# A block model in float32 on one core: the sums of the modulation vector's last four sixths, made in the wait before the token mixer instead of inside it

## Chip, cores and metric

One core of one Trainium2 chip runs one launch. The metric is device time in microseconds (us), lower is better; a run counts with the time of its only core.

## What is computed

Two blocks one after the other on 256 tokens of width 1024. The first has two layers, each attention and a squared-ReLU MLP with layer norms. The second is what the change touches: a vector c gives a modulation vector of 6 x 1024 numbers, whose sixths shift, scale and gate a token mixer and a mixture of experts.

```python
def second_block(...):
    c_act = jax.nn.silu(c)
    mod = (c_act @ w_ada[l] + b_ada[l])[:, None, :]
    sh1, sc1, g1, sh2, sc2, g2 = jnp.split(mod, 6, axis=-1)
    u = modulate(rmsnorm(h, norm1[l]), sh1, sc1)
    h = h + g1 * token_mixer(u, ...)
    u = modulate(rmsnorm(h, norm2[l]), sh2, sc2)
    h = h + g2 * hier_moe(u, ...)
    return rmsnorm(h, final_norm)
```

The mixer projects u to retention queries, keys, values and gates and to latents of a second attention, and merges both branches under two sigmoid gates; the experts are routed per token.

## The kernel before

The kernel is one program with one hand-written instruction list for each engine: `block.sync` (all weight loads), `block.gpsimd` (small and modulation loads), `block.tensor`, `block.scalar` and `block.vector`. Semaphores, named in the table `S`, tie the lists together; on each engine the instructions run in the written order. Here PE is TensorE, ACT is ScalarE, DVE is VectorE, and the order around the change is the order of the calls in those three functions.

**Weights.** Each weight block of 1 MB lands in one of four ring slots. ACT rounds it to `w_hi` (`high`, L1197), DVE writes the rest `w_lo` (`low`, L1570), and PE makes every product with three matmuls (`product`, L555 to L557) for float32-like precision. The activations come the same way: PE transposes a 128-token tile (`transposes`, L523), ACT copies it, DVE splits it to `x_hi` and `x_lo`. `tokens_out` is one projection of all 256 tokens to 1024 columns (four blocks, 96 matmuls) into the four PSUM banks of `acc`; ACT then empties the banks (`banks_out`, L1341), and the next projection waits with `freed=` for that.

**Modulation.** During both MLPs DVE accumulates c_act times the rows of w_ada in `mod` (128 partitions x 6144). The sum over the partitions is a matmul with ones. The first two sixths (shift and scale of the mixer) are needed by feature: 32 one-column matmul passes (L829) leave them in `pp` bank 0, and DVE makes `modc` from them (L1859, L1861). The last four sixths are needed by token in every partition: `mod_rows(part)` on PE multiplies a 128x512 piece of `mod` by ones into a bank of `pp` (L839, two passes for each piece, 8 pieces), and `mod_rows(part)` on ACT copies the bank back over the same piece (L1348), counting `mod_done`. Both banks of `pp` are shared. Before the change `mod_rows(0)` to `mod_rows(3)`, two pieces each, stand inside the mixer: after the projections RG (retention gate), GR and GM (the two merge gates), and RO (retention output).

**Between the second MLP and the mixer.** DVE takes the last layer norm and the RMS norm of both tiles (`last_sum`, `row_stats`, `last_norm`, `mixer_rows`), ACT takes the square roots (`norm_root`, L1308; `mixer_root`, L1362), PE transposes each tile when its `mixer_rows` is out (`r_out`), ACT applies `modc` on the way out of PSUM (`mixer_input`, L1142), DVE splits (L1557, L1558). Then the first projection of the mixer, B_C, begins. The experts come after the mixer, in a hardware loop whose weights (L397) stream while PE multiplies (L1065, L1049, L1105).

Of the kernel before, what the change touches and what calls it, by code (L numbers as in the profile page):

```python
# [27 lines left out]
LN_EPS = 1e-5  # L28
# [30 lines left out]
B_C = 96  # L59
# [44 lines left out]
def program(nc, A):  # L104
    f32, i32, f32r = mybir.dt.float32, mybir.dt.int32, mybir.dt.float32r
    ALU, ACT, AX = mybir.AluOpType, mybir.ActivationFunctionType, mybir.AxisListType
    ctx = ExitStack()
    with ctx:
# [46 lines left out]
        def con(name, rows=128):  # L155
            if name in LATE_AT:
                a, b = LATE_AT[name]
                if name == "mask":
                    return late_mask
                return stage[:, :, :].rearrange("p a b -> p (a b)")[:, a:b]  # L160
            a, b = CONST_AT[name]
            return consts[0:rows, a:b]
# [350 lines left out]
        def _(pe):  # L513
# [26 lines left out]
            def input_split():  # L540

                if groups[0] - 1 in PLAIN:
                    transposed()
                else:
                    inputs[0] += 4
                    pe.wait_ge(S["x_split"], inputs[0])
# [25 lines left out]
            def tokens_out(b, freed=None, by_tile=False, before=lambda i, j: None, cuts=(0, 512, 1024)):  # L572

                def part(i, j, q):
                    k, half = divmod(j, 2)
                    kt = 2 * i + k
                    n = cuts[half + 1] - cuts[half]
                    return product(acc[:, 2 * q + half, 0:n], x_parts(kt, slice(q * 128, (q + 1) * 128)),
                                   w_parts(b + i, k, slice(cuts[half], cuts[half + 1])),
                                   start=(kt == 0), stop=(kt == 7))  # L580

                for i in range(3 if by_tile else 4):
                    for j in range(4):
                        before(i, j)
                        if j % 2 == 0:
                            half_ready(b + i, j // 2)
                        if freed and i == 0 and j < 2:
                            pe.wait_ge(S[freed], 2 * (j + 1))
                        for q in range(QT):
                            last = part(i, j, q)  # L590
                        if j % 2 == 1:
                            last.then_inc(S["half_used"], 1)
                if by_tile:
                    before(3, 0)
                    for j in range(4):
                        if j % 2 == 0:
                            half_ready(b + 3, j // 2)
                        last = part(3, j, 0)
                    last.then_inc(S["tile_ready"], 1)
                    for j in range(4):  # L600
                        last = part(3, j, 1)
                        if j % 2 == 1:
                            last.then_inc(S["half_used"], 1)
# [226 lines left out]
                                     con("ones")[:, 0:1], start=True, stop=True)  # L830
            last.then_inc(S["mod_mm"], 1)

            def mod_rows(part):

                if part:
                    pe.wait_ge(S["mod_done"], 2 * part)
                for half in range(2):
                    at = 2048 + 1024 * part + 512 * half
                    pe.matmul(pp[:, half, :], con("ones"), mod[:, at:at + 512], start=True, stop=True)\  # L839
                        .then_inc(S["mod_mm"], 1)  # L840


            for q in range(QT):
                pe.wait_ge(S["r_out"], q + 1)
                for half in range(2):
                    transposes([(128 * j, o_tm[:, q, (4 * half + j) * 128:(4 * half + j + 1) * 128])
                                for j in range(4)])
            input_split()

            tokens_out(B_C, cuts=(0, 384, 704))  # L850

            def rqk(i):

# [17 lines left out]
            n = 0  # L871
# [108 lines left out]
            pe.wait_ge(S["rq_done"], 4)  # L980
            pe.wait_ge(S["rk_done"], 4)
            tokens_out(B_RG)
            mod_rows(0)
            tokens_out(B_GR, freed="rg_done")
            mod_rows(1)
            tokens_out(B_GM, freed="gr_done")
            mod_rows(2)
            for q in range(QT):
                pe.wait_ge(S["yret_ready"], q + 1)
                tile_to_feature_major(o_tm, q)  # L990
            input_split()
            tokens_out(B_RO, freed="gm_done")
            mod_rows(3)
            to_feature_major(o_mla)
            input_split()
            tokens_out(B_MO, freed="ret_merged")
# [126 lines left out]
        def _(act):  # L1123
# [182 lines left out]
            def norm_root(i, q):  # L1306
                act.wait_ge(S["ln_stat"], QT * i + q + 1)
                act.activation(rstd[:, q:q + 1], sr[:, q:q + 1], ACT.Sqrt).then_inc(S["ln_rstd"], 1)  # L1308
# [32 lines left out]
                        act.activation(dst[:, q, 512 * half:512 * half + 512], acc[:, 2 * q + half, :], function)\  # L1341
                            .then_inc(done, 1)

            def mod_rows(part):
                for half in range(2):
                    at = 2048 + 1024 * part + 512 * half
                    act.wait_ge(S["mod_mm"], 2 * part + half + 2)
                    act.activation(mod[:, at:at + 512], pp[:, half, :], ACT.Copy).then_inc(S["mod_done"], 1)  # L1348

            for layer in range(2):  # L1350
                attention(layer)
# [8 lines left out]
            def mixer_root(q):  # L1360
                act.wait_ge(S["r_stat"], q + 1)
                act.activation(rstd[:, q:q + 1], sr[:, q:q + 1], ACT.Sqrt).then_inc(S["r_rstd"], 1)  # L1362

            def mixer_input(*halves):
                to_input(lambda f: modc[:, 1, f:f + 1], lambda f: modc[:, 0, f:f + 1], halves)

            mixer_root(0)
            norm_root(3, 1)
            act.wait_ge(S["modc_done"], 1)
            mixer_input(0, 1)  # L1370
            mixer_root(1)
            mixer_input(0, 1)

            high(B_C + 1, n=5)
            used(B_C + 3)
            for q in range(QT):
                act.activation(lat[:, q, 0:384], acc[:, 2 * q, 0:384], ACT.Copy)
# [57 lines left out]
            used(B_RG + 3)  # L1435
            banks_out(rg, ACT.Silu, S["rg_done"])
            high(B_GR + 1)
            mod_rows(0)
            high(B_GR + 2, n=3)
            used(B_GR + 3)  # L1440
            banks_out(gate_r, ACT.Sigmoid, S["gr_done"])
            high(B_GM + 1)
            mod_rows(1)
            high(B_GM + 2, n=3)
            used(B_GM + 3)
            banks_out(gate_m, ACT.Sigmoid, S["gm_done"])
            mod_rows(2)
            to_input_plain()
            high(B_RO + 1, n=4)
            mod_rows(3)  # L1450
            to_input_plain()
            high(B_MO + 1, n=4)
            to_input_plain()
# [58 lines left out]
        def _(dve):  # L1512
# [12 lines left out]
            def used(b):  # L1525

                dve.wait_ge(S["half_used"], half_index(b, 1) + 1)
# [300 lines left out]
            def last_sum(q):  # L1828
                bank = acc[:, 2 * q:2 * q + 2, :].rearrange("p a b -> p (a b)")
                link(dve.scalar_tensor_tensor(o_tm[:, q, :], h_tm[:, q, :], ALPHA, bank, ALU.mult, ALU.add))  # L1830
# [9 lines left out]
            def mixer_rows(q):  # L1840
# [9 lines left out]
            row_stats(0, o_tm[:, 0, :], LN_EPS, S["ln_stat"])  # L1850
            last_norm(0)
            row_stats(0, h_tm[:, 0, :], EPS, S["r_stat"], rms=True)
            used(b)
            last_sum(1)
            row_stats(1, o_tm[:, 1, :], LN_EPS, S["ln_stat"])
            mixer_rows(0)

            dve.wait_ge(S["mod_mm"], 1)
            link(dve.tensor_copy(modc[:, :, :].rearrange("p a b -> p (a b)"), pp[:, 0, 0:16]))  # L1859
            at = VEC["norm1_2"][0]  # L1860
            dve.scalar_tensor_tensor(modc[:, 1, :], modc[:, 1, :], 1.0, vec[:, at:at + 8], ALU.add, ALU.mult)\  # L1861
                .then_inc(S["modc_done"], 1)
            last_norm(1)
            row_stats(1, h_tm[:, 1, :], EPS, S["r_stat"], rms=True)
            mixer_rows(1)
# [413 lines left out]
```

## Time and profile before

| what | value |
|---|---|
| median of 3 runs | 1378.13 us (1377.3 to 1379.1) |
| time of the profiled execution | 1377.12 us |
| its span in the trace | 1375.3 us |
| mean granted TensorE clock | 0.932 of full speed |
| TensorE matmul busy | 1229.9 us, 89% of the span |
| VectorE busy | 747.7 us, 54% |
| ScalarE busy | 519.3 us, 38% |
| GpSimd busy | 55.4 us, 4% |
| mean DMA rate | 208 GB/s |

Times in the trace count from the start of the span. An engine's busy time says how long it worked, not that it was waited for: that is read from the idle time before an instruction and from what ended it. A granted clock of 1.00 is TensorE at 2.4 GHz, 0.50 is 1.2 GHz.

### The profile page before, as it was taken

To read this page: it belongs to the slowest core of one execution; us is meant where nothing else is said; L and a number is where in the kernel's file an instruction comes from. 1 tells how busy PE (TensorE), PEld (TensorE's weight loads), DVE (VectorE), ACT (ScalarE), POOL (GpSimd) and SP (SyncE) were. 2 spreads that over 40 slices of the span, in tenths; PEclk is the share of its full clock that TensorE was granted. 3 is DMA by queue.
4 is the path that set the end of the run, shared out by engine and by line. 5 is a ranking of instruction groups with operands and counts; after the bars stand their busy time and mean duration, and the time that the engine had idled before them with its cause. 6 is when DMAs were issued, how large, how long until landed. Compare 5 with 4: busy or idle time off the path is not lost. (4 is left out here: it accounts for less than half of the span.)

```text
span 1375.3 us, 18670 instructions
## 1 busy us (share of the span) xinstructions
PE 1229.9 (89%) x7419; PEld 1013.4 (74%) x7419; DVE 747.7 (54%) x1256; ACT 519.3 (38%) x854; POOL 55.4 (4%) x98
## 2 busy tenths in 40 slices
PE   7788599999799869999969999999988699999994
PEld 5786489999698759999958778878766566666653
DVE  3366567777656566777775334554455722222223
ACT  3356444444445443444434322344432222222221
POOL 6000000010000000000000000000000000000000
PEclk9899789999899979999979968999998599999998
DMA  9933248788563216978724412635457199999992
GB/s 272 284 104 94 90 137 291 277 279 283 172 214 119 96 61 213 322 280 286 248 88 100 153 41 83 203 107 185 151 192 236 61 311 367 366 367 367 366 367 83
DMA packets 176069, 286.08 MB, mean 208 GB/s; under 512 B 11613, under 2 KB 137818, under 8 KB 175616
## 3 DMA queue, kind: packets, MB, share of 16 engines
q1 hardware_dynamic: 165616, 248.76, 54.1%
q0 software_dynamic: 10384, 36.37, 8.3%
q8 instruction: 46, 0.75, 0.2%
q14 instruction: 23, 0.19, 0.0%
HBM read 282.92 MB, written 2.20 MB: 207 GB/s over the span
## 5 line engine op out<-in xcount | busy, mean ns | idle before, releaser
L1570 DVE TENSOR_TENSOR w_lo<-ring,w_hi 128x1024 fp32r<-128x1024 f32 (+1 forms) x272 | 320.0, 1210 | 163.8 <-ACT w_hi L1197 156.5
L1197 ACT ACTIVATE w_hi<-ring 128x1024 fp32r<-128x1024 f32 (+1 forms) x272 | 277.9, 1050 | 180.6 <-PE acc L557 159.3
L555 PE MATMUL pp<-x_hi,w_hi 128*128 128x256 f32 x896 | 264.3, 295 | 14.3 <-DVE w_lo L1570 7.5
L556 PE MATMUL pp<-x_lo,w_hi 128*128 128x256 f32 x896 | 259.9, 290 | 0.0
L557 PE MATMUL pp<-x_hi,w_lo 128*128 128x256 f32 x896 | 259.7, 290 | 0.0
L555 PEld LDWEIGHTS pp<-x_hi,w_hi 128*128 128x128 f32 x896 | 178.5, 199 | 22.7 <-issue 14.0
L556 PEld LDWEIGHTS pp<-x_lo,w_hi 128*128 128x128 f32 x896 | 178.7, 199 | 1.4 <-issue 0.2
L557 PEld LDWEIGHTS pp<-x_hi,w_lo 128*128 128x128 f32 x896 | 178.3, 199 | 0.0
L555 PE MATMUL acc<-w_hi,x_hi 128*128 128x512 f32 (+2 forms) x384 | 156.8, 408 | 23.6 <-DVE x_lo L1544 7.1
L556 PE MATMUL acc<-w_lo,x_hi 128*128 128x512 f32 (+2 forms) x384 | 153.4, 399 | 0.0
L557 PE MATMUL acc<-w_hi,x_lo 128*128 128x512 f32 (+2 forms) x384 | 153.0, 398 | 0.0
L555 PEld LDWEIGHTS acc<-w_hi,x_hi 128*128 128x128 f32 x384 | 76.2, 198 | 45.3 <-DVE x_lo L1544 9.6
L555 PE MATMUL acc<-w_hi,hid_hi 128*128 128x512 f32 x256 | 100.0, 391 | 0.0
L556 PE MATMUL acc<-w_lo,hid_hi 128*128 128x512 f32 x256 | 100.0, 390 | 0.0
L557 PE MATMUL acc<-w_hi,hid_lo 128*128 128x512 f32 x256 | 99.6, 389 | 0.0
L557 PEld LDWEIGHTS acc<-w_hi,x_lo 128*128 128x128 f32 x384 | 75.8, 197 | 15.3
L556 PEld LDWEIGHTS acc<-w_lo,x_hi 128*128 128x128 f32 x384 | 75.9, 198 | 14.3
L1331 ACT ACTIVATE scr<-pp 128x512 f32<-128x512 f32 x32 | 19.1, 598 | 152.5 <-PE pp L557 152.5
L1793 DVE TENSOR_TENSOR scr<-scr 128x512 f32<-128x512 f32 x32 | 22.1, 692 | 81.7 <-ACT scr L1331 81.6
L1584 DVE SCALAR_TENSOR_TENSOR mod<-stage,act_c,mod 128x1024 f32<-128x1024 f32 x48 | 61.4, 1278 | 0.0
L523 PE MATMUL tp<-consts,o_tm 128*128 128x128 f32 x142 | 26.5, 341 | 38.1 <-DVE o_tm L1769 14.2
L1065 PE MATMUL pp<-ring,k_t 128*64 128x256 f32 x512 | 57.1, 379 | 3.5 <-DMA ring<-in_w_dram 3.5
(344 smaller groups left out, 1731.9 us busy)
## 6 DMA issues: line engine op xcount, KB each, us to landing
ring<-in_w_up_dram SPq DMA_DIRECT2D x32, 1024.0 KB, 5.3
ring<-in_w_down_dram SPq DMA_DIRECT2D x32, 1024.0 KB, 6.9
ring<-in_w_dram SPq DMA_DIRECT2D x32, 1024.0 KB, 12.7
stage<-in_w_ada_dram POOLq DMA_DIRECT2D x48, 512.0 KB, 6.5
ring<-in_w_in_dram SPq DMA_DIRECT2D x24, 1024.0 KB, 5.1
big<-in_w_dram SPq DMA_DIRECT2D x24, 1024.0 KB, 11.2
ring<-in_w_in_a_dram SPq DMA_DIRECT2D x12, 1024.0 KB, 14.0
ring<-in_w_kv_shared_dram SPq DMA_DIRECT2D x8, 1024.0 KB, 5.8
```

What stands on the lines that cost most here:

```text
L523: last = pe.transpose(tp[:, g % 2, off:off + 128], src, ident)
L555: pe.matmul(out, lhs[0], rhs[0], start=start, stop=False)
L556: pe.matmul(out, lhs[0], rhs[1], start=False, stop=False)
L557: return pe.matmul(out, lhs[1], rhs[0], start=False, stop=stop)
L1065: last = pe.matmul(up_bank[64 * e:64 * e + 64, 256 * w:256 * w + 256], xe[:, kt, x], e_ring[6 * pair + 2 * w + e][:, 256 * kt:256 * kt + 256],
L1197: act.activation(shaped(high_half(bb, k), raw), raw, ACT.Copy).then_inc(S["hi_ready"], 1)
L1331: act.activation(relu[:, v % 2, :], pp[:, v % 2, :], ACT.Relu).then_inc(S["relu_done"], 1)
L1570: dve.tensor_tensor(shaped(low_half(bb, k), raw), raw, shaped(high_half(bb, k), raw), ALU.subtract).then_inc(S["lo_ready"], 1)
L1584: dve.scalar_tensor_tensor(part, stage[:, i % 2, :], act_c[:, k:k + 1], part, ALU.mult, ALU.add)\
L1793: dve.tensor_tensor(h, h, h, ALU.mult).then_inc(S["sq_done"], 1)
```

## The change

PE's and ACT's `mod_rows` take a range of pieces instead of a sixth's number, and alternate the banks of `pp` starting with bank 1. On PE the pieces 0 and 1 come right after the one-column matmuls, 2 to 6 between the transposes of tile 0 and tile 1, 7 after those of tile 1; piece 1 waits for `modc_done`, since bank 0 holds the sums for `modc` until then. On ACT the copies 0 and 1 stand ahead of the last `norm_root`, 2 to 6 between the modulated copies of tile 0 and the square root of tile 1, 7 between the first and the second block of B_C. On DVE `modc` and `mixer_rows(0)` move ahead of `last_sum(1)`. The four calls inside the mixer go, and PE waits for all eight copies before it next writes `pp`.

```diff
--- before.py
+++ after.py
@@ -830,24 +830,28 @@
                                      con("ones")[:, 0:1], start=True, stop=True)
             last.then_inc(S["mod_mm"], 1)
 
-            def mod_rows(part):
-
-                if part:
-                    pe.wait_ge(S["mod_done"], 2 * part)
-                for half in range(2):
-                    at = 2048 + 1024 * part + 512 * half
-                    pe.matmul(pp[:, half, :], con("ones"), mod[:, at:at + 512], start=True, stop=True)\
+            def mod_rows(start, end):
+
+                for i in range(start, end):
+                    if i == 1:
+                        pe.wait_ge(S["modc_done"], 1)
+                    elif i >= 2:
+                        pe.wait_ge(S["mod_done"], i - 1)
+                    at = 2048 + 512 * i
+                    pe.matmul(pp[:, (i + 1) % 2, :], con("ones"), mod[:, at:at + 512], start=True, stop=True)\
                         .then_inc(S["mod_mm"], 1)
 
-
+            mod_rows(0, 2)
             for q in range(QT):
                 pe.wait_ge(S["r_out"], q + 1)
                 for half in range(2):
                     transposes([(128 * j, o_tm[:, q, (4 * half + j) * 128:(4 * half + j + 1) * 128])
                                 for j in range(4)])
+                mod_rows(2 + 5 * q, 7 + q)
             input_split()
 
             tokens_out(B_C, cuts=(0, 384, 704))
+            pe.wait_ge(S["mod_done"], 8)
 
             def rqk(i):
 
@@ -980,17 +984,13 @@
             pe.wait_ge(S["rq_done"], 4)
             pe.wait_ge(S["rk_done"], 4)
             tokens_out(B_RG)
-            mod_rows(0)
             tokens_out(B_GR, freed="rg_done")
-            mod_rows(1)
             tokens_out(B_GM, freed="gr_done")
-            mod_rows(2)
             for q in range(QT):
                 pe.wait_ge(S["yret_ready"], q + 1)
                 tile_to_feature_major(o_tm, q)
             input_split()
             tokens_out(B_RO, freed="gm_done")
-            mod_rows(3)
             to_feature_major(o_mla)
             input_split()
             tokens_out(B_MO, freed="ret_merged")
@@ -1341,11 +1341,12 @@
                         act.activation(dst[:, q, 512 * half:512 * half + 512], acc[:, 2 * q + half, :], function)\
                             .then_inc(done, 1)
 
-            def mod_rows(part):
-                for half in range(2):
-                    at = 2048 + 1024 * part + 512 * half
-                    act.wait_ge(S["mod_mm"], 2 * part + half + 2)
-                    act.activation(mod[:, at:at + 512], pp[:, half, :], ACT.Copy).then_inc(S["mod_done"], 1)
+            def mod_rows(start, end):
+
+                for i in range(start, end):
+                    at = 2048 + 512 * i
+                    act.wait_ge(S["mod_mm"], i + 2)
+                    act.activation(mod[:, at:at + 512], pp[:, (i + 1) % 2, :], ACT.Copy).then_inc(S["mod_done"], 1)
 
             for layer in range(2):
                 attention(layer)
@@ -1365,13 +1366,16 @@
                 to_input(lambda f: modc[:, 1, f:f + 1], lambda f: modc[:, 0, f:f + 1], halves)
 
             mixer_root(0)
+            mod_rows(0, 2)
             norm_root(3, 1)
             act.wait_ge(S["modc_done"], 1)
             mixer_input(0, 1)
+            mod_rows(2, 7)
             mixer_root(1)
             mixer_input(0, 1)
-
-            high(B_C + 1, n=5)
+            high(B_C + 1)
+            mod_rows(7, 8)
+            high(B_C + 2, n=4)
             used(B_C + 3)
             for q in range(QT):
                 act.activation(lat[:, q, 0:384], acc[:, 2 * q, 0:384], ACT.Copy)
@@ -1435,19 +1439,15 @@
             used(B_RG + 3)
             banks_out(rg, ACT.Silu, S["rg_done"])
             high(B_GR + 1)
-            mod_rows(0)
             high(B_GR + 2, n=3)
             used(B_GR + 3)
             banks_out(gate_r, ACT.Sigmoid, S["gr_done"])
             high(B_GM + 1)
-            mod_rows(1)
             high(B_GM + 2, n=3)
             used(B_GM + 3)
             banks_out(gate_m, ACT.Sigmoid, S["gm_done"])
-            mod_rows(2)
             to_input_plain()
             high(B_RO + 1, n=4)
-            mod_rows(3)
             to_input_plain()
             high(B_MO + 1, n=4)
             to_input_plain()
@@ -1850,16 +1850,15 @@
             row_stats(0, o_tm[:, 0, :], LN_EPS, S["ln_stat"])
             last_norm(0)
             row_stats(0, h_tm[:, 0, :], EPS, S["r_stat"], rms=True)
-            used(b)
-            last_sum(1)
-            row_stats(1, o_tm[:, 1, :], LN_EPS, S["ln_stat"])
-            mixer_rows(0)
-
             dve.wait_ge(S["mod_mm"], 1)
             link(dve.tensor_copy(modc[:, :, :].rearrange("p a b -> p (a b)"), pp[:, 0, 0:16]))
             at = VEC["norm1_2"][0]
             dve.scalar_tensor_tensor(modc[:, 1, :], modc[:, 1, :], 1.0, vec[:, at:at + 8], ALU.add, ALU.mult)\
                 .then_inc(S["modc_done"], 1)
+            mixer_rows(0)
+            used(b)
+            last_sum(1)
+            row_stats(1, o_tm[:, 1, :], LN_EPS, S["ln_stat"])
             last_norm(1)
             row_stats(1, h_tm[:, 1, :], EPS, S["r_stat"], rms=True)
             mixer_rows(1)
```

The list of PE's instructions between the second MLP and the first projection of the mixer (L841 is L839 before, the pieces' matmuls; L523 the transposes of `o_tm`):

```order
 L829 MATMUL pp<-consts,mod 128x1 x16
-L523 MATMUL tp<-consts,o_tm 128x128 x16
+L841 MATMUL pp<-mod,consts 128x512 x2
+L523 MATMUL tp<-consts,o_tm 128x128 x8
+L841 MATMUL pp<-mod,consts 128x512 x5
+L523 MATMUL tp<-consts,o_tm 128x128 x8
+L841 MATMUL pp<-mod,consts 128x512
 L555 MATMUL acc<-w_hi,x_hi 128x384
```

All eight pieces now stand ahead of B_C: two before the first tile's transposes, five between the tiles, one after.

The same place on ACT (L1349 is L1348 before, a piece's copy; L1363 is L1362 before, the root of the mixer's norm; L1308 the root of the layer norm; L1142 the modulated copies of a tile):

```order
 L1308 ACTIVATE rstd<-sr 128x1
-L1362 ACTIVATE rstd<-sr 128x1
+L1363 ACTIVATE rstd<-sr 128x1
+L1349 ACTIVATE mod<-pp 128x512 x2
 L1308 ACTIVATE rstd<-sr 128x1
 L1142 ACTIVATE scr<-tp,modc 128x128 x8
-L1362 ACTIVATE rstd<-sr 128x1
+L1349 ACTIVATE mod<-pp 128x512 x5
+L1363 ACTIVATE rstd<-sr 128x1
 L1142 ACTIVATE scr<-tp,modc 128x128 x8
```

The root of tile 1 followed the modulated copies of tile 0 directly; now five copies, each of which needs its matmul, stand between them.

ACT inside the mixer, from the emptying of GR's banks (first row) over GM's to the copies that start RO's input (last row):

```order
 L1341 ACTIVATE big<-acc 128x512 x4
-L1197 ACTIVATE w_hi<-ring 128x1024 x2
-L1348 ACTIVATE mod<-pp 128x512 x2
-L1197 ACTIVATE w_hi<-ring 128x1024 x6
+L1197 ACTIVATE w_hi<-ring 128x1024 x8
 L1341 ACTIVATE big<-acc 128x512 x4
-L1348 ACTIVATE mod<-pp 128x512 x2
 L1172 ACTIVATE x_hi<-tp 128x4x128 x4
```

The copies of pieces no longer stand between the emptying of GM's banks and the first copy of RO's input.

## Rows read from the trace of the kernel before

**Rows 1.** Chain of waits, mixer and experts: start us, us, what:

```profile
922.70 1.72 PE pp L839 x4
...
1099.39 7.13 PE pp L1065 x64
...
1296.25 11.86 DMA ring<-in_w_dram
```

**Rows 2.** Timeline of PE, MLP to mixer: start, us, operation, [idle before <-releaser]:

```profile
694.08 4.03 PE L829 MATMUL pp<-consts,mod 128*128 128x1 f32 x32
703.31 1.97 PE L523 MATMUL tp<-consts,o_tm 128*128 128x128 f32 x8 [5.20 <-DVE o_tm L1842]
709.34 1.97 PE L523 MATMUL tp<-consts,o_tm 128*128 128x128 f32 x8 [4.06 <-DVE o_tm L1842]
714.69 0.69 PE L555 MATMUL acc<-w_hi,x_hi 128*128 128x384 f32 x1 [3.38 <-DVE x_lo L1558]
```

**Rows 3.** Timeline of DVE, the same stretch:

```profile
699.46 1.20 DVE L1830 SCALAR_TENSOR_TENSOR o_tm<-h_tm,acc 128x1024 f32<-128x1024 f32 x1
...
702.52 0.73 DVE L1842 TENSOR_SCALAR o_tm<-h_tm,rstd 128x1024 f32<-128x1024 f32 x1
703.17 0.17 DVE L1859 COPY modc<-pp 128x16 f32<-128x16 f32 x1
...
708.53 0.75 DVE L1842 TENSOR_SCALAR o_tm<-h_tm,rstd 128x1024 f32<-128x1024 f32 x1 [0.27 <-ACT rstd L1362]
```

**Rows 4.** Timeline of ACT, the same stretch:

```profile
699.57 0.20 ACT L1362 ACTIVATE rstd<-sr 128x1 f32<-128x1 f32 x1 [4.50 <-DVE sr L1756]
702.64 0.20 ACT L1308 ACTIVATE rstd<-sr 128x1 f32<-128x1 f32 x1 [2.86 <-DVE sr L1756]
704.55 2.90 ACT L1142 ACTIVATE scr<-tp,modc 128x128 f32<-128x128 f32 x8 [1.71 <-PE tp L523]
708.29 0.20 ACT L1362 ACTIVATE rstd<-sr 128x1 f32<-128x1 f32 x1 [0.85 <-DVE sr L1756]
...
718.29 0.80 ACT L1197 ACTIVATE w_hi<-ring 128x704 fp32r<-128x704 f32 x1 [3.48 <-PE acc L557]
```

**Rows 5.** Windows: us, busy (x) of PE, PEld, DVE, ACT, POOL, then PEclk, DMA:

```profile
698.00:703.00 5.00, 0.12 (x1) 0.03 (x1) 4.72 (x13) 0.41 (x2) 0.00 (x0) 0.50 0.00 0
...
714.69:717.60 2.91, 2.91 (x10) 2.91 (x11) 1.55 (x2) 0.12 (x1) 0.00 (x0) 0.50 0.10 12
```

**Rows 6.** Timeline of PE, end of RG to GR:

```profile
922.53 1.88 PE L839 MATMUL pp<-mod,consts 128*128 128x512 f32 x4
...
924.48 0.40 PE L556 MATMUL acc<-w_lo,x_hi 128*128 128x512 f32 x1
924.72 0.40 PE L557 MATMUL acc<-w_hi,x_lo 128*128 128x512 f32 x1
```

**Rows 7.** Timeline of ACT, end of RG to GR:

```profile
922.73 2.07 ACT L1341 ACTIVATE big<-acc 128x512 f32<-128x512 f32 x4 [3.08 <-PE acc L557]
```

**Rows 8.** Timeline of ACT, end of GM to RO:

```profile
971.72 1.12 ACT L1348 ACTIVATE mod<-pp 128x512 f32<-128x512 f32 x2
972.68 1.15 ACT L1172 ACTIVATE x_hi<-tp 128x512 fp32r<-128x512 f32 x2
```

**Rows 9.** Timeline of PE, first matmuls of RO, and where they speed up:

```profile
976.84 0.66 PE L555 MATMUL acc<-w_hi,x_hi 128*128 128x512 f32 x1 [1.48 <-DVE x_lo L1544]
980.28 0.47 PE L557 MATMUL acc<-w_hi,x_lo 128*128 128x512 f32 x1
```

**Rows 10.** Timeline of DVE, end of RO to MO:

```profile
1000.53 2.48 DVE L2002 TENSOR_TENSOR q_t<-acc,big 128x512 f32<-128x512 f32 x4 [3.13 <-PE acc L557]
1003.36 1.29 DVE L1544 TENSOR_TENSOR x_lo<-tp,x_hi 128x512 fp32r<-128x512 f32 x2 [0.35 <-ACT x_hi L1172]
```

**Rows 11.** Timeline of PE, end of RO to MO:

```profile
1000.33 1.88 PE L839 MATMUL pp<-mod,consts 128*128 128x512 f32 x4
...
1006.77 0.50 PE L555 MATMUL acc<-w_hi,x_hi 128*128 128x512 f32 x1 [1.41 <-DVE x_lo L1544]
```

## Prediction

> **What bounds the kernel now.** I read the chain of waits first: it tells which engine's work sets the end. In the mixer it runs through PE, with the piece matmuls on it: four passes after RG are 1.72 us of it [rows 1]. So each of the eight pieces, two passes each, looks like 0.86 us of path. In the experts the chain is PE's passes over the streamed weights and late in the loop a wait of 11.86 us for a load [rows 1]. Both begin with the loop at 1099.39, so what the mixer gains or loses arrives at the end unchanged.
>
> Then the stretch between second MLP and mixer, on three engines. PE ends its one-column sums at 694.08 + 4.03 = 698.11 and starts B_C at 714.69; between them are two groups of transposes, each released by DVE's `mixer_rows` [rows 2]. DVE is the bound: only 0.27 us idle stands before its last `mixer_rows`, released by ACT's root [rows 3]. ACT idles 4.50, 2.86, 1.71 and 0.85 us before its steps there [rows 4]. PE's clock is at half speed, 0.50, from 698, and B_C's first 2.91 us run at it too [rows 5]. This is the space into which the pieces go.
>
> **What leaves the mixer.** Each removal is costed by what PE would wait for without it.
>
> After RG: PE cannot write the first banks of GR before ACT has emptied two. ACT starts at 922.73; four copies in 2.07 us at 0.60 us each [rows 7] (the last begins 1.47 us after the first, 0.49 us apart) put the second's end at 922.73 + 0.49 + 0.60 = 923.8, and GR could start at about 923.9. Now the pieces stream from 922.53, and GR's second pass starts at 924.48, 0.24 us before its third [rows 6], so the first effectively at 924.25. Gain 0.35 us, not 1.72: the pieces stood in a wait for PSUM that would be there without them. After GR the pattern is the same: 0.35 us.
>
> After GM, PE's next need is RO's input, which ACT copies. ACT's two piece copies start at 971.72, the first copy of RO's input at 972.68 [rows 8]. Without them the latter moves up 0.96 us, and DVE's split and RO with it: 0.96 us.
>
> After RO, DVE has four merges from 1000.53, 2.48 us, ending at 1003.0, and the first split starts at 1003.36 after a wait of 0.35 us for ACT's copy, itself behind the two piece copies [rows 10]. Without them DVE goes on at 1003.0: 0.35 us.
>
> Sum: 0.35 + 0.35 + 0.96 + 0.35 = **2.0 us off**. Bounds: 1.2 us (the first two give nothing, if emptying costs some tenths more) and 2.6 us.
>
> **What comes into the wait.** DVE's work is the same in another order. `modc` and `mixer_rows(0)` stand before `last_sum(1)`, which starts at 699.46 now, so `mixer_rows(0)` starts near 699.9 instead of 702.52 [rows 3]. Its transposes could follow at 700.7, were PE not busy with piece 1. Step by step:
> - PE: piece 0 from 698.1; piece 1 only after `modc`, 699.9. A piece is 0.86 us at full clock, so an estimated 1.72 at half. At half: both done at 701.6, transposes of tile 0 (1.97 us, rows 2) to 703.6.
> - ACT: root at 699.57, two copies (0.60 us each) by 702.4. The next root waits for tile 1's statistics. They come now at 702.64 - 0.04 = 702.60 [rows 4] and later by `mixer_rows(0)` and `modc`, some 1.0 us: root done 703.85. Then the eight modulated copies, 2.90 us [rows 4]: 706.8.
> - Pieces 2 and 3 are in their banks by 707.1 at the latest; ACT's copies free the first bank at 707.4. Piece 4 therefore starts at 707.45, whatever the clock, and 4, 5, 6 follow each other.
> - At full clock: 707.45 + 3 x 0.86 = 710.0, then the last copy and the root, 0.2 + 0.6 + 0.2: 711.0. At half: 707.45 + 3 x 1.72 = 712.6, root done 713.6. Today the root is done at 708.29 + 0.20 = 708.49 [rows 4].
>
> Behind that root everything of tile 1 queues: DVE's `mixer_rows(1)`, and on DVE behind it the splits of both tiles, then PE and B_C, 6.2 us from root to B_C today (708.49 to 714.69, rows 4 and 2) and then. So B_C starts **2.5 us later at full clock, 5.1 at half**. The trace has the clock low in all of this stretch, but pieces 2 and 3 give PE 3.4 us of dense work, and B_C's start shows the clock rising after 2.91 us of such [rows 5]. I take one of the three waiting pieces at half and two at full: 3.4 us. PE and ACT, idle there today, become the bound.
>
> Piece 7 costs nothing: PE has it while DVE splits tile 1, ACT in the 3.48 us idle before B_C's second block [rows 4]. PE's wait for eight copies comes after B_C's 96 matmuls and is met. Loads are issued in the same order and follow the weights' use; none is moved.
>
> **The clock.** Pieces were PE's dense work in its pauses. RO's first nine passes start from 976.84 to 980.28 at half clock, 0.43 us apart instead of 0.23 [rows 9]: 1.6 us lost. MO, after a like pause, starts at nearly full clock: its first pass takes 0.50 [rows 11]. Its last piece ends at 1000.33 + 1.72 = 1002.05 today, 4.7 us ahead of MO [rows 11]. Without pieces the last dense pass ends at 1000.5 and MO starts at about 1006.4: 5.9 us of transposes and idleness. RO's pause today is at least 4.6 us, from the start of the second piece's copy at 972.2 [rows 8] to 976.84. Ends: nothing, or RO's loss, 1.6 us. The nearest row is RO's, but MO's own says it may hold: I take 0.9 us. At B_C's start, low for 2.91 us today, the ends are no change and a gain of 1.45 us. The Trainium skill says ("TensorE: Matmul & The Clock Gate", section "Why this matters for your kernels") that long idle gaps between bursts of matmuls drop the clock and that keeping PE busy holds it up. By that rule B_C would start at full clock, and the sum would be 1.45 us lower. Row against it: transposes and a tail of DVE work of 6.2 us still lie between piece 6 and B_C, as long as the pause after which RO is slow, so I take no change.
>
> **Sum**: 3.4 - 2.0 + 0.9 + 0 = +2.3 us. The profiled execution took 1377.12 us and would take 1379.4; the median of the runs shown, 1378.13, is 1.0 above it, so against the median the forecast is **1380.4 us**. A measurement of this kernel can tell about 0.2%, 2.8 us, from no change.
>
> **Rivals.**
> 1. Slow clock throughout. The three waiting pieces run at half speed (+5.1) and MO starts slow (+1.6), with 2.0 off: +4.7 us, **1382.8**. For it: 0.50 in the whole stretch now. It decides if ACT's last root before B_C ends later than 712 and MO's first passes are 0.43 apart.
> 2. The pieces keep the clock up. Waiting pieces at full clock (+2.5), B_C at full clock from its start (-1.45), MO unharmed, 2.0 off: -0.95 us, **1377.2**, no change to a measurement. It decides if the granted clock is 1.00 when B_C starts. Against it: the 6.2 us tail. It is what the rule of the Trainium skill named above would make of this stretch.
> 3. The pieces were real path and the wait hides the new ones better than my steps say. PE's eight pieces come off in full, 8 x 0.86 = 6.9 us, with +3.4 in the wait: -3.5 us, **1374.6**, faster. The chain of waits speaks for it [rows 1]; ACT's emptying that ends at 923.8 speaks against it [rows 7]. It decides if GR starts as soon as RG ends.
> 4. The change doesn't do what it says (`modc` or a bank not free, so pieces queue in B_C): PE would idle after B_C for the eighth copy. Nothing in the rows makes that copy late; priced at up to +2 us more, it is inside rival 1's range.
>
> **Chances.** Forecast 0.50, of which 0.30 lies within 0.2% and 0.20 above; rival 1 (with 4) 0.22; rival 2 0.14; rival 3 0.14. Faster by over 0.2%: 0.14. Within: 0.30 + 0.14 = 0.44. Slower: 0.20 + 0.22 = 0.42. The range for 8 in 10 runs from just below rival 2 to above rival 1 with its bounds (5.1 - 1.2 + 1.6 = +5.5): **1376.0 to 1383.8**; it leaves out most of rival 3.
>
> **What would show it.** Right: in the stretch before B_C, idle of DVE before its last `mixer_rows` grows from 0.27 to 2.5 to 5 us, ended by ACT's root; that root stands behind five piece copies; GR and GM start about 1.4 us after the projection before them instead of 1.7, PE idle between; RO's first input copy follows the emptying directly; MO's first passes are slower. Wrong: the gap from the end of the MLP to B_C no longer than today, or PE running through from RG to GR without a pause, or the clock at 1.00 at B_C's start.

## The result, and the profile after

The changed kernel takes **1383.83 us** (median of 7 runs, 1382.52 to 1385.56), the kernel before in the same session 1377.30 us (7 runs). The ratio is 1.0049, 95% interval 1.0037 to 1.0061: 6.5 us slower. The profiled execution took 1383.83 us with a span of 1382.0 us, 6.7 us over the span before; mean granted clock 0.930.

Section 1 of the page of the changed kernel, busy us and share of the span:

```profile
PE 1237.2 (90%) x7419; PEld 1016.6 (74%) x7419; DVE 748.5 (54%) x1256; ACT 519.9 (38%) x854; POOL 55.4 (4%) x98
```

Every engine ran as many instructions as before, but PE's are 7.3 us longer in sum, more than the whole difference. That already points at PE's clock, not only at waits.

Timeline of PE, end of the second MLP to B_C, in the changed kernel (to be held against [rows 2]; L841 are the pieces):

```profile
694.68 3.63 PE L829 MATMUL pp<-consts,mod 128*128 128x1 f32 x32
698.17 1.10 PE L841 MATMUL pp<-mod,consts 128*128 128x512 f32 x2
700.48 2.08 PE L841 MATMUL pp<-mod,consts 128*128 128x512 f32 x2 [1.20 <-DVE modc L1856]
702.34 1.92 PE L523 MATMUL tp<-consts,o_tm 128*128 128x128 f32 x8
704.05 2.89 PE L841 MATMUL pp<-mod,consts 128*128 128x512 f32 x4
707.81 2.94 PE L841 MATMUL pp<-mod,consts 128*128 128x512 f32 x6 [0.87 <-ACT mod L1349]
712.32 1.10 PE L523 MATMUL tp<-consts,o_tm 128*128 128x128 f32 x8 [1.57 <-DVE o_tm L1842]
...
717.50 0.69 PE L555 MATMUL acc<-w_hi,x_hi 128*128 128x384 f32 x1 [3.22 <-DVE x_lo L1558]
```

The first row starts 0.60 us later than before, ahead of anything the change touches. From there to B_C it is 22.82 us, before 20.61: **2.2 us** more. Pieces 4 to 6 (x6) wait for ACT's copies.

Timeline of ACT between the tiles, and DVE's last `mixer_rows` (against [rows 4] and [rows 3]):

```profile
707.13 1.12 ACT L1349 ACTIVATE mod<-pp 128x512 f32<-128x512 f32 x2
708.98 0.60 ACT L1349 ACTIVATE mod<-pp 128x512 f32<-128x512 f32 x1 [0.73 <-PE pp L841]
709.84 0.60 ACT L1349 ACTIVATE mod<-pp 128x512 f32<-128x512 f32 x1 [0.26 <-PE pp L841]
710.79 0.60 ACT L1349 ACTIVATE mod<-pp 128x512 f32<-128x512 f32 x1 [0.36 <-PE pp L841]
711.28 0.19 ACT L1363 ACTIVATE rstd<-sr 128x1 f32<-128x1 f32 x1
...
711.51 0.76 DVE L1842 TENSOR_SCALAR o_tm<-h_tm,rstd 128x1024 f32<-128x1024 f32 x1 [2.55 <-ACT rstd L1363]
```

The chain of the prediction is there link by link: the root of tile 1 stands behind five copies, and DVE's idle time before its last `mixer_rows` grew from 0.27 to 2.55 us.

Windows of the changed kernel: from the copies of pieces 2 and 3 on (first row), the pieces between the tiles, the last 1.2 us before B_C, then B_C's, RO's and MO's first passes, and the last weight load's matmuls (columns as in [rows 5]; the figure after POOL's is the clock):

```profile
706.10:716.30 10.20, 5.74 (x18) 2.11 (x16) 6.62 (x15) 6.97 (x19) 0.54 (x1) 1.00 0.07 19
709.00:712.00 3.00, 1.75 (x4) 0.30 (x2) 0.49 (x1) 1.86 (x4) 0.00 (x0) 1.00 0.00 0
716.30:717.50 1.20, 0.00 (x0) 0.00 (x1) 1.17 (x3) 1.20 (x3) 0.00 (x0) 0.51 0.00 0
...
717.50:723.10 5.60, 5.60 (x18) 5.60 (x19) 2.34 (x3) 1.39 (x3) 0.00 (x0) 0.50 0.53 158
978.20:982.60 4.40, 4.36 (x10) 3.47 (x11) 2.36 (x2) 1.15 (x2) 0.00 (x0) 0.50 0.20 19
1008.20:1013.30 5.10, 5.04 (x12) 3.98 (x13) 2.37 (x3) 1.17 (x2) 0.00 (x0) 0.50 0.19 48
1347.60:1351.20 3.60, 3.60 (x18) 2.55 (x20) 0.00 (x0) 0.00 (x0) 0.00 (x0) 0.53 0.77 306
```

The clock is at 1.00 while the waiting pieces run and down again before B_C begins. B_C's passes are slow for 5.6 us (before 2.91, [rows 5]), RO's for 4.4 (before 3.4), MO's for 5.1 where before they began almost at speed [rows 11].

Timeline of PE in the mixer: the last pass of RG and the first two of GR, then around the inputs of RO and MO:

```profile
924.73 0.39 PE L557 MATMUL acc<-w_hi,x_lo 128*128 128x512 f32 x1
926.39 0.47 PE L555 MATMUL acc<-w_hi,x_hi 128*128 128x512 f32 x1 [1.27 <-ACT big L1341]
926.70 0.40 PE L556 MATMUL acc<-w_lo,x_hi 128*128 128x512 f32 x1
...
971.58 1.03 PE L523 MATMUL tp<-consts,o_tm 128*128 128x128 f32 x8
975.21 1.62 PE L523 MATMUL tp<-consts,o_tm 128*128 128x128 f32 x8 [2.59 <-DVE x_lo L1544]
978.24 0.80 PE L555 MATMUL acc<-w_hi,x_hi 128*128 128x512 f32 x1 [1.41 <-DVE x_lo L1544]
...
1002.13 1.03 PE L523 MATMUL tp<-consts,mod 128*128 128x128 f32 x8
1005.46 1.38 PE L523 MATMUL tp<-consts,mod 128*128 128x128 f32 x8 [2.30 <-DVE x_lo L1544]
1008.26 0.80 PE L555 MATMUL acc<-w_hi,x_hi 128*128 128x512 f32 x1 [1.41 <-DVE x_lo L1544]
```

Where pieces stood after RG, PE now idles 1.27 us until ACT has emptied the banks. RO begins 6.66 us after GM's passes (978.24 - 971.58), before 7.24 (976.84 less 969.60, where the pieces began); MO 6.13 after RO's, before 6.44 [rows 11]. The last RG pass and the first GR pass of the kernel before, for the comparison:

```profile
922.30 0.40 PE L557 MATMUL acc<-w_hi,x_lo 128*128 128x512 f32 x1
...
923.96 0.68 PE L555 MATMUL acc<-w_hi,x_hi 128*128 128x512 f32 x1
```

The 6.7 us add up along PE's list. Each row is the time from the start of one marked pass to the start of the next, read from the timelines of both traces (differences from the unrounded times):

| stretch | before | changed | difference |
|---|---|---|---|
| start of the span to the one-column sums | 694.1 | 694.7 | +0.6 |
| to B_C's first pass | 20.6 | 22.8 | +2.2 |
| to the first matmul of UQ (B_C, RQK) | 32.5 | 33.7 | +1.2 |
| to the last matmul of retention | 152.4 | 150.8 | -1.6 |
| to RO's first pass (RG, GR, GM) | 77.3 | 76.2 | -1.0 |
| to MO's first pass (RO) | 29.9 | 30.0 | +0.1 |
| to WO's first pass (MO) | 31.1 | 33.5 | +2.3 |
| to the router's first matmul (WO) | 31.6 | 32.4 | +0.8 |
| to the experts' first matmul | 29.8 | 30.3 | +0.4 |
| to the experts' last weight matmul | 246.5 | 248.1 | +1.7 |
| to the end of the span | 29.4 | 29.5 | 0.0 |

From retention to the router the pieces were taken off, and the stretch became 2.1 us longer (170.0 to 172.1).

### The profile page after: what moved, and what is told of

It is laid out like the page before. It is cut to its first block and busy times, and to the rows that moved or that the text cites. A ratio compares the mean times of both kernels' runs of the same rounds, so it can differ in the third digit from the quotient of the medians.

```text
span 1382.0 us, 18671 instructions
## 1 busy us (share of the span) xinstructions
PE 1237.2 (90%) x7419; PEld 1016.6 (74%) x7419; DVE 748.5 (54%) x1256; ACT 519.9 (38%) x854; POOL 55.4 (4%) x98
## 5 line engine op out<-in xcount | busy, mean ns | idle before, releaser
L2180 DVE SCALAR_TENSOR_TENSOR w_lo<-tp,slot_gate,w_hi 128x512 fp32r<-128x512 f32 x32 | 24.0, 751 | 66.3 <-ACT w_hi L1496 42.6
```

The lines of the kernel that those rows point to most:

```text
L2180: dve.scalar_tensor_tensor(y_lo[:, half, :], y_bank[half], slot_gate[:, 0:1], y_hi[:, half, :], ALU.mult, ALU.subtract).then_inc(S[f"y{hal ...
```

## The experiments

The questions: is it the wait or the clock, and what did the pieces in the mixer really cost? All ratios are against runs of the kernel before on the same chip.

**No pieces at all.** The calls of `mod_rows` go from PE and ACT, and DVE's wait for them. This kernel leaves the last four sixths of the vector unsummed, so its output is not the model's; it serves for timing alone:

```diff
             tokens_out(B_RG)
-            mod_rows(0)
             tokens_out(B_GR, freed="rg_done")
-            mod_rows(1)
             tokens_out(B_GM, freed="gr_done")
-            mod_rows(2)
...
-            dve.wait_ge(S["mod_done"], 8)
```

> The kernel before with the eight pieces left out on PE and ACT altogether (the last four sixths of the modulation vector are not summed over the partitions; nothing takes their place in the wait). Theory A, clock: the pieces in the mixer cost only 2.0 us of path, and they kept the clock up in the pauses before RO and MO, so that without them both start at half clock more often: 0 to +3 us against before, with a granted clock of 0.5 at MO's first passes. Theory B, the wait alone: taking them out of the mixer gains its 2 us and the clock's differences there are chance: -2 us. Theory C, the pieces were real path: -6.9 us.

1381.16 us against 1377.76, ratio 1.0018 (1.0006 to 1.0031). Eight matmuls and eight copies less, and the kernel is not faster but slower, by 2.5 us. In its trace RO and MO both start at half clock, and the way from retention to the router is 172.2 us, as in the changed kernel (172.1) and not as before (170.0). This is theory A's outcome; B and C are out. One part of its time has nothing to do with PE: behind the last instruction of DVE the span goes on for 3.1 us, in the kernel before for 4.0. The other kernel without pieces shows the same, all ten kernels with pieces are like before. Why the store of the output ends sooner there is not shown. Without this 1.0 us the loss would be about 3.5 us.

**The changed kernel with its pauses filled.** Six matmuls into an unused bank:

```diff
+            def fill(count):
+                for _ in range(count):
+                    pe.matmul(pp[:, 0, :], con("ones"), mod[:, 2048:2560], start=True, stop=True)
...
             for q in range(QT):
                 pe.wait_ge(S["yret_ready"], q + 1)
                 tile_to_feature_major(o_tm, q)
+                fill(2 - q)
             input_split()
             tokens_out(B_RO, freed="gm_done")
-            to_feature_major(o_mla)
+            for q in range(QT):
+                tile_to_feature_major(o_mla, q)
+                fill(2 - q)
             input_split()
```

> The changed kernel with six matmuls whose result is not used in PE's pauses before RO and MO (two after tile 0's transposes, one after tile 1's). Theory A, the clock: RO and MO start at full clock, 2.5 to 4 us less than the changed kernel, +2.5 to +4 against before. Theory B, the clock in the mixer does not matter: as the changed kernel, +6.5, or a little more for the matmuls.

1377.27 us against 1377.76, ratio 0.9997 (0.9985 to 1.0009): work whose result nobody reads takes back all of the change's loss, about 7 us, more than the 2.5 to 4 expected. Windows over RO's and MO's first passes in its trace:

```profile
981.00:985.00 4.00, 3.96 (x17) 3.27 (x18) 2.36 (x2) 1.90 (x3) 0.00 (x0) 1.00 0.24 20
1009.00:1014.00 5.00, 5.00 (x22) 4.16 (x23) 3.17 (x3) 2.16 (x3) 0.00 (x0) 1.00 0.27 54
```

The clock is 1.00 in both, and retention to router takes 166.3 us instead of 172.1: 5.8 us of the gain lie in this stretch. The transposes of tile 1 ran faster too, so each input was there earlier. Not all of the 5.8 us were lost by the change: RO was slow in the kernel before as well, and the fill repairs that too.

**Both: pieces in the wait and in the mixer.** The changed kernel's wait, its copies put into an unused tile, and the four calls in the mixer restored:

```diff
-                    act.activation(mod[:, at:at + 512], pp[:, (i + 1) % 2, :], ACT.Copy).then_inc(S["mod_done"], 1)
+                    act.activation(big[:, 512 * (i % 2):512 * (i % 2) + 512], pp[:, (i + 1) % 2, :], ACT.Copy)\
+                        .then_inc(S["dm_done"], 1)
...
             tokens_out(B_RG)
+            mod_rows(0)
             tokens_out(B_GR, freed="rg_done")
```

> The changed kernel's work in the wait before the mixer, with its copies put in an unused tile, and besides the pieces in the mixer as they were before: the cost of the wait alone. Theory A: B_C starts 2.2 us later (the root of tile 1 behind five copies), a little more through the clock at B_C's start: +2 to +4 us against before. Theory B: +6 to +8 us, all of the change's loss.

1384.44 us against 1377.76, ratio 1.0039 (1.0021 to 1.0057), with runs from 1377.5 to 1387.8. In the profiled execution (1380.60) one-column sums to B_C take 22.83 us as in the changed kernel, and retention to router 169.7, as before. So the trace puts the wait's own cost at 2.2 us, and B_C's passes are 1.2 us longer. The ratio's interval reaches from 2.9 to 7.9 us: it overlaps both the +2 to +4 of theory A and the +6 to +8 of theory B, so the time of this kernel does not tell them apart; the trace and the two experiments above do. What made the slower runs slower is not in this one trace.

**The root first.**

```diff
-            mod_rows(2, 7)
             mixer_root(1)
+            mod_rows(2, 7)
```

> The changed kernel with ACT's root of tile 1 ahead of the copies 2 to 6, nothing else. The late root's theory: ACT no longer holds DVE, but PE still has pieces 4 to 6 ahead of tile 1's transposes and ends them at about 710.7, where the transposes could start at 709.9; B_C starts about 1 us earlier than in the changed kernel, time +5.5 us against before. If it is the root alone that counts, B_C starts 2.2 us earlier, +4.3. If the root is not what holds B_C, no difference, +6.5.

1385.44 us against 1377.76, ratio 1.0054 (1.0040 to 1.0069): no gain over the changed kernel, where about 1 us was expected. The timeline of PE says why:

```profile
710.32 2.94 PE L841 MATMUL pp<-mod,consts 128*128 128x512 f32 x6 [3.54 <-ACT mod L1349]
713.10 1.04 PE L523 MATMUL tp<-consts,o_tm 128*128 128x128 f32 x8
...
717.95 0.44 PE L555 MATMUL acc<-w_hi,x_hi 128*128 128x384 f32 x1 [2.95 <-DVE x_lo L1558]
```

ACT now waits for the root's input before it copies, PE's pieces 4 to 6 wait 3.54 us for the copies, and the transposes of tile 1 stand behind them on PE. From the one-column sums to B_C it is 22.67 us. I had costed PE's part as if the copies still ran early. In both orders the pieces between the tiles hold tile 1: once in ACT's list, once in PE's.

**DVE's new order alone.** `modc` and `mixer_rows(0)` ahead of `last_sum(1)` in the kernel before:

```diff
+            dve.wait_ge(S["mod_mm"], 1)
+            link(dve.tensor_copy(modc[:, :, :].rearrange("p a b -> p (a b)"), pp[:, 0, 0:16]))
...
+            mixer_rows(0)
             used(b)
             last_sum(1)
```

> The kernel before with DVE's new order alone (modc and mixer_rows(0) ahead of last_sum(1)), all pieces where they were. DVE does the same work before its last root, so B_C should start as before: 0 us, within 0.1%. If the order itself costs (ACT's copies of tile 0 wait for the later layer-norm root), B_C starts up to 1 us later and the change's loss in the wait is not all the pieces': +1.

1378.86 us against 1378.99, ratio 1.0000 (0.9991 to 1.0010), and 20.7 us to B_C. The order is free; the 2.2 us are the pieces'. B_C's slow passes are another matter. In this kernel's trace, with no piece in the wait, they last longer than in the changed kernel:

```profile
716.20:722.40 6.20, 6.20 (x21) 6.20 (x22) 2.44 (x3) 0.91 (x2) 0.00 (x0) 0.50 0.55 169
```

**The kernel before with RO's and MO's pauses filled**, behind the pieces:

```diff
                 tile_to_feature_major(o_tm, q)
+                pe.wait_ge(S["mod_done"], 6)
+                fill(2 - q)
...
+                tile_to_feature_major(o_mla, q)
+                pe.wait_ge(S["mod_done"], 8)
+                fill(1)
```

> The kernel before, pieces kept, with unused matmuls in PE's pauses before RO (two and one) and MO (one and one). Clock theory: RO and MO start at full clock in every execution; before lost 1.6 us at RO in the profiled one and something at MO in others: -1.5 to -3 us against before. If the fill of the changed kernel gained by something else than the clock: 0 or slightly positive.

1378.09 us against 1378.99, ratio 0.9992 (0.9978 to 1.0005): unclear, smaller than expected. RO started at full clock, but two fills after the pieces no longer fitted: GM's passes to RO take 7.73 us instead of 7.24, and retention to router 169.4 against 170.0. Of the 1.6 us gained in RO's passes 0.5 went back as this delay, and 0.5 in WO's passes, which were slow for longer.

**The kernel before with B_C's pause filled.**

```diff
+            fill(2)
             for q in range(QT):
                 pe.wait_ge(S["r_out"], q + 1)
...
+                fill(2)
             input_split()
```

> The kernel before with unused matmuls in PE's pauses between second MLP and B_C alone (two after the one-column sums, two after each tile's transposes). Clock theory: transposes at full clock bring B_C some 0.5 us forward and its first passes lose nothing: -1.5 to -3 us. If a fill at half clock runs over its pause, it delays the transposes: 0 to +1.

1375.58 us against 1378.99, ratio 0.9979 (0.9965 to 0.9993): 2.9 us faster. In the profiled execution the transposes of tile 1 run at full clock (1.10 us instead of 1.97), yet B_C comes only 0.2 us earlier, and 3.4 us of its passes are slow in this one too. The time gained stands; that it comes from B_C's clock is not shown by this trace.

**A version meant to beat both.** The pieces after RG and GR stay, the last four serve as filler behind the transposes, and ACT copies them after the input:

```diff
+            def piece(i, count):
+                pe.wait_ge(S["mod_done"], i - 1)
+                for _ in range(count):
+                    last = pe.matmul(pp[:, i % 2, :], con("ones"), mod[:, 2048 + 512 * i:2560 + 512 * i],
+                                     start=True, stop=True)
+                last.then_inc(S["mod_mm"], 1)
...
                 tile_to_feature_major(o_tm, q)
+                piece(4 + q, 2 - q)
...
                 tile_to_feature_major(o_mla, q)
+                piece(6 + q, 2 - q)
...
+            fill(2)
             for q in range(QT):
                 pe.wait_ge(S["mla_merged"], q + 1)
                 tile_to_feature_major(merged, q)
+                fill(1)
...
+            to_input_plain()
             mod_rows(2)
+            high(B_RO + 1, n=4)
             to_input_plain()
-            high(B_RO + 1, n=4)
             mod_rows(3)
-            to_input_plain()
```

(The last part is ACT's. B_C's pause is filled as above.)

> A version meant to beat both: the pieces after RG and GR stay in the wait for ACT's emptying, the last four go behind the transposes of RO's and MO's input, the first of each pair twice as filler, their copies behind the input's copies on ACT; B_C's and WO's pauses are filled too. From the parts: RO and MO start 1.2 us earlier (0.96 + 0.35, less the fill's tail), no clock loss at RO and MO (-2), B_C (-2), WO (-1.5): -4 to -7 us against before. If pieces only cost by their number, it would be at best -1.

**1370.45 us** against 1378.99, ratio 0.9940 (0.9925 to 0.9954): 8.3 us faster than the kernel before, beyond the expected 4 to 7. Timeline of PE around RO's input, and windows over RO's, MO's and WO's first passes:

```profile
967.38 1.03 PE L523 MATMUL tp<-consts,o_tm 128*128 128x128 f32 x8
968.25 1.88 PE L997 MATMUL pp<-mod,consts 128*128 128x512 f32 x4
971.00 1.16 PE L523 MATMUL tp<-consts,o_tm 128*128 128x128 f32 x8 [0.87 <-DVE x_lo L1562]
972.00 1.02 PE L997 MATMUL pp<-mod,consts 128*128 128x512 f32 x2
973.64 0.50 PE L555 MATMUL acc<-w_hi,x_hi 128*128 128x512 f32 x1 [0.61 <-DVE x_lo L1562]
```

```profile
973.60:978.00 4.40, 4.36 (x19) 3.63 (x20) 2.51 (x3) 3.13 (x4) 0.00 (x0) 1.00 0.00 0
1001.50:1006.00 4.50, 4.46 (x20) 3.69 (x21) 2.61 (x3) 3.19 (x4) 0.00 (x0) 1.00 0.00 0
1031.00:1036.00 5.00, 4.39 (x19) 3.35 (x19) 3.26 (x4) 2.94 (x4) 0.00 (x0) 1.00 1.04 405
```

RO begins 6.26 us after GM's passes, all three projections start at full clock, and PE still idles 0.87 and 0.61 us behind its filler, so nothing waits for that. Retention to router is 164.4 us, 5.6 less than before. This kernel changes several things at once, so its 8.3 us are not divided further here.

**No pieces, pauses filled**, and **the changed kernel again** beside it:

```diff
             tokens_out(B_RG)
-            mod_rows(0)
...
                 tile_to_feature_major(o_tm, q)
+                fill(2 - q)
```

> The first experiment (no pieces anywhere; the last four sixths are not summed) with the six unused matmuls before RO and MO: its distance to the changed kernel with the same fill is the cost of the pieces in the wait, without the clock at RO and MO. By the trace: B_C 2.2 us later and up to 1.3 us of slow passes there, so this kernel should be 2 to 4 us faster than the filled changed kernel: -2.5 to -4.5 us against before. If it is no faster than that (about -0.5), the wait costs nothing and all of the change's loss is the clock in the mixer; if it is at -6 or below, the wait costs more than the trace shows.

> The changed kernel itself again, on the same chip as the one above: +5 to +8 us against before, so that both differences (fill, pieces in the wait) stand beside it. If its loss were chance of the first runs, it would come within 2 us of before.

1374.02 us against 1378.47, ratio 0.9971 (0.9960 to 0.9981), and 1385.68 against 1378.47, ratio 1.0056 (1.0040 to 1.0072). With the results above this is a square of four kernels, in us against before:

| | pauses at RO and MO empty | filled |
|---|---|---|
| no pieces anywhere | +2.5 | -4.0 |
| pieces in the wait before B_C | +7.7 | -0.4 |

(ratio less one, times the median before; each is good to 1.5 to 2.2 us). Filling the pauses is worth 6.5 and 8.1 us. The difference between the rows is 5.2 and 3.6; 1.0 us of it is the output's store, which ends sooner in both kernels without pieces, so the pieces in the wait cost about 4.2 and 2.6. The two effects are separate and, within the noise, add.

What the clock did to the three projections is read from the traces: the time from a projection's first pass to its last, each of 96 passes, in us.

| kernel | RO | MO | WO | retention to router |
|---|---|---|---|---|
| before | 23.25 | 21.68 | 23.53 | 170.0 |
| changed | 23.66 | 24.01 | 24.29 | 172.1 |
| no pieces | 23.83 | 24.11 | 24.33 | 172.2 |
| both | 23.17 | 21.66 | 23.39 | 169.7 |
| changed, filled | 21.71 | 21.67 | 23.29 | 166.3 |
| no pieces, filled | 21.67 | 21.65 | 23.43 | 166.4 |
| version meant to beat both | 21.66 | 21.66 | 21.67 | 164.4 |

At full clock a projection takes 21.7 us. All four traces without pieces in the mixer and without fill (changed, no pieces, root first, changed again) have 172.1 to 172.2 us in the last column, all four with the pieces there and these pauses not filled (before, both, order alone, B_C filled) 169.7 to 170.0.

## Why the prediction was wrong

- **What leaves the mixer: right in place, too high in size.** Forecast 2.0 us, measured 1.3. After RG the first pass of GR is recorded 1.66 us behind RG's last in both kernels, but before it took 0.68 us and now 0.47; by the second pass, as the prediction counted, the gain is 0.2 us (2.18 against 1.97; forecast 0.35), and after GR the same. After GM it is 0.58 (forecast 0.96; the clock fell in the pause and the second transposes took 1.62 us), after RO 0.31 (forecast 0.35). The chain of waits had shown 1.72 us of pieces after RG [rows 1], and almost all of it stood in place of a wait for PSUM, as [rows 7] said. Rival 3 is refuted.
- **What comes into the wait: right, somewhat high.** Forecast +3.4 with ends 2.5 and 5.1, measured +2.2. The three waiting pieces all ran at full clock, where one was taken at half, and the first of them began 0.2 us ahead of the steps by hand. The order-alone kernel shows that it is the pieces, and the root-first kernel that ACT's list is not the only thing that holds tile 1.
- **The clock in the mixer: the step that failed.** The sum had +0.9 us for it, at MO alone, with an end of 1.6. Measured against the kernel before it was **3.5 us**: RO's passes +0.4, MO's +2.3, WO's +0.8 (the table of projections). Less the 1.3 us of removals this is the 2.1 us (from unrounded times) by which the stretch from retention to the router grew. Three things were missed. MO's start at full clock was taken as likely to hold by half; it was gone in all four traces that had neither pieces nor fill there. RO's loss of 1.6 us was taken as what a fall costs, but MO's is 2.3: its slow stretch is 5.1 us long. And RO, slow already, became slower (4.4 us instead of 3.4), and WO, behind both, too; neither had a term. The fill and the both-kernel show that it is the clock and that the pieces in the mixer had held it up: with either, MO takes 21.7 us.
- **B_C's clock: forecast no change, in this trace +1.2 us, cause not shown.** The clock rose during the waiting pieces (1.00 from 706 to 716 us) and was at half again 1.2 us before B_C. The slow passes lasted 5.6 us instead of 2.9. But in the order-alone kernel, without pieces there, they lasted 6.2 us, and in two of the five traces with pieces 3.4. So one trace of each kernel does not tell whether the pieces lengthened them. The Trainium skill's advice ("TensorE: Matmul & The Clock Gate", "Why this matters for your kernels") is to keep pauses between bursts of matmuls short. At RO and MO the traces agree with it: with the pauses filled both start at 1.00, without pieces or fill at 0.50. Ahead of B_C the change left the last pause as it was, 3.22 us idle against 3.38 before, so the advice did not promise a full clock there, as the prediction read it. Rival 2 had the clock's rise with the pieces right and expected it to last until B_C, which it did not. In the mixer the same advice of the Trainium skill spoke against the change, and there I gave it half of one fall.
- **Not foreseen.** From the router to the experts' loop the four traces without pieces in the mixer and without fill take 30.2 to 30.3 us, the four with the pieces and these pauses not filled 29.8: +0.4, which probably belongs to the clock as well. The passes behind the last weight load ran at half clock for 3.4 us in the changed kernel (+1.7), and did so in five of the other executions, with and without pieces in the wait; the kernel before did not in its one trace. That part and the 0.6 us ahead of the change I do not count to the change.
- **The numbers.** The forecast was a rise of 2.3 us, measured are 6.5; 1383.83 lies 0.03 us above the range. Of the trace's 6.7 us, the wait is 2.2, the removals -1.3, the clock at RO, MO and WO 3.5; the other 2.3 are B_C's passes, the stretches that differ between executions, and the 0.4 before the experts. That the total came so near to the end of the range, and to rival 1 (1382.8), is partly luck: rival 1 had +5.1 in the wait and +1.6 at MO.

What stays open is what the wait costs in all. The square puts it at 2.6 to 4.2 us, the traces at 2.2 and perhaps a part of B_C's passes. The stretch from B_C's first pass to the end of retention could hold the rest: it takes 184.5 or 186.6 us in the five traces with pieces in the wait and 181.7 to 184.9 in the other seven. One trace of each kernel doesn't settle that, and in the pair of the change itself it went the other way (184.9 before, 184.5 changed).

## What to carry to other kernels

Before taking matmuls out of a stretch, ask what PE would wait for without them: here the pieces filled waits for PSUM and for another engine's split, and taking them out gave 1.3 us, a fifth of their 6.9. Dense matmuls next to a pause also kept the clock up here for the projection behind it. If such work has to go, try something else right before the projection, behind the last transposes, and on the copying engine behind the critical copies. Work put into another engine's wait should not stand in the list ahead of the short instruction that ends that wait.

## What was unexpected of the hardware

Six matmuls with an unused result, 12 passes of 0.43 us at full clock and so 5.2 us of PE time, made a 1384 us kernel about 7 us shorter. And how long the clock stays low behind a pause is not settled by the work alone: after the same pieces and the same pause B_C's passes were slow for 5.6 us in the changed kernel's trace and for 3.4 in that of the filled kernel, there after a start at full clock. Without pieces it was 2.9 us in the kernel before and 6.2 in the order-alone kernel.
